# Two skewed streams of 512-token tiles, with weights cast once to bf16 in DRAM, in a two-layer hybrid encoder

## The chip, the cores and the metric

The kernel runs on the 8 cores of one Trainium2 chip. Each core takes two of the sixteen sequences, 4096 tokens in all, and runs the same program; no core waits for another. The metric is the device time of the slowest core, in microseconds.

## What is computed

x is (16, 2048, 1024) float32. Layer 0 mixes tokens by windowed attention, layer 1 by a gated short convolution; each is followed by a gated MLP whose gate goes through a width-3 convolution over positions.

```
def _conv_glu_ffn(h, w_gate_up, conv_w, w_down):
    gu = h @ w_gate_up                                   # (B, S, 2*D_FF), D_FF = 2816
    g, u = jnp.split(gu, 2, axis=-1)
    return (jax.nn.silu(_dwconv3(g, conv_w)) * u) @ w_down

def _short_conv_mixer(h, w_in, conv_w, w_out):
    b_gate, c_gate, xv = jnp.split(h @ w_in, 3, axis=-1)
    return (b_gate * _dwconv3(c_gate * xv, conv_w)) @ w_out

for i in range(2):
    hn = _rmsnorm(h, g_pre_mix)
    mix = _windowed_gqa(hn, ...) if i == 0 else _short_conv_mixer(hn, ...)
    h = h + _rmsnorm(mix, g_post_mix)
    f = _conv_glu_ffn(_rmsnorm(h, g_pre_ffn), ...)
    h = h + _rmsnorm(f, g_post_ffn)
```

Attention has 16 query and 4 key heads of width 64, rotary positions, a band of 128 tokens to each side and a learned sink.

## The kernel before

Activations lie channels by tokens, 128 channels a chunk, 8 chunks. The tokens of a core are cut in four stages of 1024 tokens; a stage is two tiles of 512 tokens (the last stage: three of 342). Both tiles of a stage go through the same steps one behind the other and share every weight that is loaded:

1. `wo_stage`: the attention's output projection (8 matmuls per chunk and tile), norm, residual from `xT`, result to the DRAM tensor `hd`.
2. `ffn` of layer 0: `pre_norm`, then 22 times a gate unit and an up unit of 8 matmuls each (`proj`), `conv3`, silu and product into `act`; then `down`, 22 matmuls per output chunk.
3. `conv_layer`: `pre_norm`, 8 times three units of 8 matmuls, then `down` with 8 matmuls per chunk.
4. `ffn` of layer 1, whose `down` writes the output `yT`.

Each of the four ends in `down` (L736 to L776) with the same tail, called a stage boundary here: the norm's factor `rs` on ScalarE, then for each of 8 chunks of each tile a residual load `hl` (256 KB, from `xT` or `hd`), a multiply and an add on VectorE, and a store of the chunk (256 KB); the next `pre_norm` squares the chunks, sums them on TensorE (`ones`), and scales them on VectorE, and only then can the next projections run. All of the tile's stages use one `x` and one `act` buffer.

Weights are float32 in DRAM. `load_w` (L463) loads a unit through GpSimd's DMA queue, which casts it to bf16 on the way, into a ring `w` of six. Residual loads, stores and attention's inputs `xs` are issued by SyncE (SP).

QKV projections and attention of the next stage's tiles are side work: `spread` (L883) gives them due times between those of the main line, on two PSUM banks of their own. The order on every engine is made by `Graph.schedule` (L182): a list scheduler with modelled durations that takes, on each engine, the ready operation with the earliest due time `vt`. ScalarE has a penalty of 15 for an operation that needs another function table. The program keeps that order: an engine runs its instructions strictly one after the other and waits for semaphores in place, and so does a queue's issuer.

The convolution needs tokens of the neighbour tile: `conv3` copies two columns in (`gs<-hs`) and two out (`hs<-gs`) for each tile and unit, on VectorE (L706, L708).

Attention for tiles 0 and 1 is all done before the first stage starts.

## Time and profile before

| | |
|---|---|
| three runs | 3545.93, 3550.9, 3839.99 us; median 3550.9 |
| the profiled execution | 3548.72 us; the span of its slowest core (core 3) 3547.2 us |
| spans of the eight cores | 3509.2 to 3547.2 us |
| busy, of the span | TensorE 89%, VectorE 55%, ScalarE 50%, GpSimd 12% |
| mean granted clock of TensorE | 0.929 of full speed on core 3 |

TensorE (PE) is the busiest engine. A busy share is a mean over stages of very different kinds, so the rows further down are cut by stage. The granted clock has two levels in the records, 1.0 (2.4 GHz) and 0.5 (1.2 GHz); a fraction between them is a window that holds both. "Share" of DMA is the mean busy share of the core's 16 DMA engines. GB/s counts bytes written: a load that casts float32 to bf16 reads twice of what it is counted for.

### The profile page before, as it was taken

To read this page: it belongs to the slowest core of one execution; us is meant where nothing else is said; L and a number is where in the kernel's file an instruction comes from. 1 tells how busy PE (TensorE), PEld (TensorE's weight loads), DVE (VectorE), ACT (ScalarE), POOL (GpSimd) and SP (SyncE) were. 2 spreads that over 40 slices of the span, in tenths; PEclk is the share of its full clock that TensorE was granted. 3 is DMA by queue.
4 is the path that set the end of the run, shared out by engine and by line. 5 is a ranking of instruction groups with operands and counts; after the bars stand their busy time and mean duration, and the time that the engine had idled before them with its cause. 6 is when DMAs were issued, how large, how long until landed. Compare 5 with 4: busy or idle time off the path is not lost.

```text
span 3547.2 us, 49902 instructions; the slowest of 8 cores (3509.2 to 3547.2 us)
## 1 busy us (share of the span) xinstructions
PE 3145.1 (89%) x14720; PEld 1406.1 (40%) x14720; DVE 1947.3 (55%) x4030; ACT 1774.4 (50%) x3095; POOL 425.1 (12%) x807
## 2 busy tenths in 40 slices
PE   3598999888998799897999799988999699888995
PEld 1212444333433344342443234433343256554663
DVE  3443771747724674465752577174872477175742
ACT  1276554455555455445556354445555565335641
POOL 1100111111110111010111011111111011110110
PEclk8757999999999899898999899989999899998997
DMA  6803574656547756646654965465543855555544
GB/s 146 164 6 85 111 130 68 144 87 126 79 62 172 164 95 110 137 75 140 117 95 57 201 127 76 65 146 94 120 74 55 177 106 76 90 127 138 82 73 113
DMA packets 219624, 382.13 MB, mean 108 GB/s; under 512 B 26210, under 2 KB 60002, under 8 KB 219362
## 3 DMA queue, kind: packets, MB, share of 16 engines
q0 software_dynamic: 115200, 205.57, 39.1%
q1 hardware_dynamic: 104162, 173.37, 17.8%
q8 instruction: 126, 2.06, 0.2%
q14 instruction: 136, 1.11, 0.1%
HBM read 516.47 MB, written 67.90 MB: 165 GB/s over the span
## 4 chain that ended last, share of the span: by engine, by line
PE 75%; DMA 11%; DVE 5%; ACT 4%; issue 3%; SPq 1%; DVEq 0%; ACTq 0%; POOLq 0%
PE ps L294 75%; DMA hl<-hd 5%; DVE x L307 3%; DMA xs<-xT 2%; DVE x L317 1%; DMA yT<-x 1%; DMA hl<-xT 1%; DMA tabd<-t 1%; ACT rs L303 1%; ACT pt L303 1%; DMA cosT<-tabd 1%; ACT rec L303 1%; SPq L329 1%; ACT sq L303 1%; DVE gc L317 0%
## 5 line engine op out<-in xcount | busy, mean ns | idle before, releaser
L294 PE MATMUL ps<-x,w 128*128 128x512 bf16 (+3 forms) x8064 | 1648.4, 359 | 30.0 <-DVE x L317 19.2
L294 PEld LDWEIGHTS ps<-x,w 128*128 128x128 bf16 x8064 | 783.7, 98 | 834.2 <-issue 116.5
L294 PE MATMUL ps<-act,w 128*128 128x512 bf16 (+6 forms) x3744 | 800.2, 356 | 0.1
L317 DVE SCALAR_TENSOR_TENSOR gc<-gs,cst_sb,gc 128x512 f32<-128x512 f32 (+9 forms) x1018 | 659.6, 653 | 136.4 <-ACT gc L303 91.6
L294 PEld LDWEIGHTS ps<-act,w 128*128 128x128 bf16 x3744 | 354.2, 98 | 329.9 <-issue 33.7
L303 ACT ACTIVATE gc<-gs,cst_sb 128x512 f32<-128x512 f32 (+6 forms) x468 | 312.0, 670 | 180.9 <-DVE gs L321 161.9
L303 ACT ACTIVATE gs<-ps 128x512 f32<-128x512 f32 (+3 forms) x396 | 215.0, 545 | 282.7 <-PE ps L294 273.1
L303 ACT ACTIVATE sq<-ps 128x512 bf16<-128x512 f32 (+6 forms) x280 | 157.1, 562 | 389.2 <-PE ps L294 388.8
L303 ACT ACTIVATE act<-gc 128x512 bf16<-128x512 f32 (+5 forms) x396 | 229.8, 583 | 238.8 <-DVE gc L317 141.8
L294 PE MATMUL ps<-sq,ones 128*128 128x512 bf16 (+7 forms) x496 | 195.9, 397 | 149.0 <-ACT sq L303 145.7
L329 POOL DMA_DIRECT2D w<-wgu x352 | 185.8, 528 | 1164.0 <-PE ps L294 1163.9
L307 DVE TENSOR_TENSOR act<-act,ps 128x512 bf16<-128x512 bf16 (+5 forms) x396 | 248.1, 629 | 131.9 <-ACT act L303 88.3
L307 DVE TENSOR_TENSOR x<-x,rs 128x512 f32<-128x512 f32 (+6 forms) x280 | 166.4, 640 | 255.9 <-ACT rs L303 255.7
L303 ACT ACTIVATE pt<-ps 128x512 bf16<-128x512 f32 x368 | 214.8, 598 | 73.3 <-PE ps L294 69.5
L307 DVE TENSOR_TENSOR x<-x,hl 128x512 f32<-128x512 f32 (+6 forms) x280 | 177.7, 642 | 115.8 <-DMA hl<-hd 94.9
L294 PE MATMUL ps<-hns,wq 128*128 128x512 bf16 x640 | 185.9, 405 | 47.7 <-DVE hns L317 20.0
L307 DVE TENSOR_TENSOR q<-ps,rec 64x512 bf16<-64x512 f32 x128 | 87.4, 683 | 232.6 <-PE ps L294 122.8
L303 ACT ACTIVATE x<-ps,cst_sb 128x512 f32<-128x512 f32 (+6 forms) x280 | 181.8, 650 | 42.8 <-DMA yT<-x 40.8
L303 ACT ACTIVATE sq<-x 128x512 bf16<-128x512 f32 (+4 forms) x216 | 122.9, 581 | 159.7 <-DVE x L307 147.7
L294 PE MATMUL ps<-q,k 64*128 64x512 bf16 x368 | 160.6, 445 | 22.5 <-ACT pt L303 15.2
L329 POOL DMA_DIRECT2D w<-wd x192 | 101.3, 528 | 640.2 <-PE ps L294 640.2
L307 DVE TENSOR_TENSOR pt<-pt,mhi 128x512 bf16<-128x512 bf16 x120 | 50.9, 424 | 221.5 <-ACT pt L303 221.0
(69 smaller groups left out, 1967.9 us busy)
## 6 DMA issues: line engine op xcount, KB each, us to landing
w<-wgu POOLq DMA_DIRECT2D x352, 256.0 KB, 4.6
hd<-x SPq DMA_DIRECT2D x144, 256.0 KB, 5.5
xs<-xT SPq DMA_DIRECT2D x128, 256.0 KB, 6.2
w<-wd POOLq DMA_DIRECT2D x128, 256.0 KB, 4.1
hl<-hd SPq DMA_DIRECT2D x120, 256.0 KB, 6.9
w<-win POOLq DMA_DIRECT2D x96, 256.0 KB, 4.6
wq<-wqk POOLq DMA_DIRECT2D x80, 256.0 KB, 5.7
hl<-xT SPq DMA_DIRECT2D x64, 256.0 KB, 7.2
```

The lines of the kernel that those rows point to most:

```text
L294: return lambda e: e.matmul(out, lhsT=lhsT, rhs=rhs, start=start, stop=stop)
L303: return lambda e: e.activation(out=out, in_=in_, func=func, **kw)
L307: return lambda e: e.tensor_tensor(out=out, in0=in0, in1=in1, op=o)
L317: return lambda e: e.scalar_tensor_tensor(out=out, in0=in0, scalar=scalar, in1=in1, op0=o0, op1=o1)
L329: return lambda e: e.dma_start(out=out, in_=in_)
```

## The change

- The 4096 tokens are eight tiles of 512 tokens. Even tiles are stream 0, odd tiles stream 1. Each stream has its own `x`, `act`, conv buffers, three PSUM banks and a ring of five weight buffers, and loads every weight for each tile. The due times set stream 1 behind stream 0 by 28 us of its own matmul time (56 us where both run). The last tile is cut into two parts of 258 and 254 tokens.
- 188 DMAs on GpSimd's queue cast all weights once, from DRAM to bf16 tensors in DRAM, eight in flight: the ninth waits for the first. Weights are then loaded as bf16 by SP (`load_w`), except those of attention for the first tiles, which are not cast yet and still come through `load_f32`.
- The copies of edge columns go from VectorE to GpSimd.
- Attention of tile 1 and the QKV of tile 2 get due times beside the start of stream 0. The residual buffers `hl` are now the conv buffers of the stream; `xs` has two buffers in place of four.
- The penalty for a new function table is 3 in place of 15 except for attention's exponentials. In the scheduler's model each DMA queue has a rate of its own, 230 GB/s, where one of 260 was shared.
- `down` starts its matmuls on each third of a chunk's weights as it comes.

```
+XW = 516
+SKEW = 28.0
...
-                key = hp[0][0] + (15.0 if tab is not None and tab != table else 0.0)
+                key = hp[0][0] + (hp[0][2].pen if tab is not None and tab != table else 0.0)
...
-                dma_free = max(dma_free, e.free) + o.nbytes / 260e3
-                fin = dma_free + 2.0
+                fin = max(dma_free.get(e, 0.0), e.free) + o.nbytes / 230e3
+                dma_free[e] = fin
+                fin += 2.0
...
-        x = sb("x", [128, NCH, XW], F32)
-        xbf = x[:, :, :].bitcast(BF16)
-        act = sb("act", [128, NFF, XW], BF16)
-        hl_r = ring("hl", 4, [128, 512], F32, True)
-        gs_r = ring("gs", 3, [128, GSW], F32)
-        gc_r = ring("gc", 2, [128, 512], F32)
...
+        class Stream:
+            def __init__(self, i):
+                self.i = i
+                self.x = sb(f"x{i}_", [128, NCH, XW], F32)
+                self.xbf = self.x[:, :, :].bitcast(BF16)
+                self.act = sb(f"act{i}_", [128, NFF, XW], BF16)
+                self.gs = ring(f"gs{i}_", 2, [128, XW], F32, True)
+                self.yc = ring(f"gc{i}_", 2, [128, 512], F32, True)
+                self.hl = Ring([self.gs.items[0], self.yc.items[0], self.gs.items[1], self.yc.items[1]])
+                self.w = ring(f"w{i}_", 5, [128, 1024], BF16, True)
+                self.sq = ring(f"sq{i}_", 2, [128, 512], BF16)
+                self.rs = ring(f"rs{i}_", 1, [128, 512], F32)
+                self.xB = [[Buf() for _ in range(2)] for _ in range(NCH)]
+                self.actB = [[Buf() for _ in range(2)] for _ in range(NFF)]
+                self.frontB = [Buf() for _ in range(2)]
+                self.st = [[dsem(f"d_st{i}_{c}_{p}") for p in range(2)] for c in range(NCH)]
...
-        xs_r = ring("xs", 4, [128, 512], F32, True)
+        xs_r = ring("xs", 2, [128, 512], F32, True)
...
+        castB = {}
+
+        def cast_w(key, i, dst, src, n):
+            castB[key] = Buf()
+            op(POOL, f_dma(dst, src), 0.55, [], [castB[key]], dsem=cast_sems[i % 8], nbytes=512 * n)
+
+        def load_w(rg, key, src, n):
             it = rg.next()
-            op(POOL, f_dma(it.ap[:, 0:n], src), 0.55, [], [it.buf], dsem=it.dsem, nbytes=512 * n)
+            op(SP, f_dma(it.ap[:, 0:n], src), 0.06, [castB[key]], [it.buf], dsem=it.dsem, nbytes=256 * n)
+            return it
+
+        def load_f32(rg, src, n):
+            it = rg.next()
+            op(POOL, f_dma(it.ap[:, 0:n], src), 0.55, [], [it.buf], dsem=it.sw, nbytes=512 * n)
             return it
 
         def mm(out, lhsT, rhs, first, last, reads, wbuf, n):
...
+                        rb = [b for c in range(NCH) for b in st.xcells(c, pv.col, pv.col + pn)]
+                    op(POOL, f_copy(st.xbf[:, :, 2 * c0:2 * c0 + 1], src), 0.3, rb + cur, [st.frontB[si]])
...
+        def edge_in(ge, src, hrow):
+            op(POOL, f_copy(src.ap[:, 0:2], hs[:, hrow, :]), 0.3, [hsB[hrow]], [src.edge])
+
         def conv3(ge, src, hrow, wcol):
 
             s, n, na = src.ap, ge.n, ge.na
-            op(DVE, f_copy(s[:, 0:2], hs[:, hrow, :]), 0.12, [hsB[hrow]], [src.buf])
             if ge.w1 < NTOK:
-                op(DVE, f_copy(hs[:, hrow, :], s[:, n:n + 2]), 0.12, [src.buf], [hsB[hrow]])
+                op(POOL, f_copy(hs[:, hrow, :], s[:, n:n + 2]), 0.3, [src.buf], [hsB[hrow]])
             else:
-                op(DVE, f_memset(s[:, n + 2:n + 3], 0.0), 0.1, [], [src.buf])
+                op(POOL, f_memset(s[:, n + 2:n + 3], 0.0), 0.3, [src.buf], [src.edge])
             b0 = ge.sh + 1
-            y = gc_r.next()
+            y = ge.st.yc.next()
             d = y.ap
-            op(ACT, f_act(d[:, 0:na], s[:, b0 + 1:b0 + 1 + na], AF.Copy, scale=wcol(1)), t_act(na, True),
-               [src.buf, cstB], [y.buf])
+            rd = [src.buf, src.edge, cstB]
...
+        def down(st, subs, ph_lag, l, gj, nk, wsrc, movs, res, dst):
 
             info = []
-            for si, sub in enumerate(subs):
+            for sub in subs:
                 a0, a1 = sub.win(ph_lag)
-                info.append((sub, a0, a1 - a0, sub.pool.get()))
+                info.append((sub, a0, a1 - a0, st.pool.get()))
             for m in range(NCH):
-                slots = []
+                bks = [st.pool.get() for _ in subs]
                 for k0 in range(0, nk, 8):
                     kn = min(8, nk - k0)
-                    slots.append(load_w(w_r, wsrc(m, k0, kn), kn * 128))
-                for si, (sub, a0, n, ss) in enumerate(info):
+                    sl = load_w(st.w, *wsrc(m, k0, kn), kn * 128)
+                    for bk, (sub, a0, n, ss) in zip(bks, info):
+                        for k in range(k0, k0 + kn):
+                            for (lo, hi, mv, mb) in movs(sub, k, a0, n):
+                                mm(bk.ap[:, lo:hi], sl.ap[:, (k - k0) * 128:(k - k0) * 128 + 128], mv, k == 0,
+                                   k == nk - 1, [sl.buf] + mb, bk.buf, hi - lo)
+                    yield kn * t_mm(512)
+                for bk, (sub, a0, n, ss) in zip(bks, info):
...
+                    hl = st.hl.next()
+                    for (dst_ap, src_ap, nb, rb) in res(c, a0, n, hl.ap):
+                        op(SP, f_dma(dst_ap, src_ap), 0.06, rb, [hl.buf, hl.edge], dsem=hl.dsem, nbytes=nb)
...
+        def stream(st):
+            for t in range(st.i, 8, 2):
+                if t < 7:
+                    subs = [Sub(t, 512 * t, 512 * t + 512, 0, st.pool)]
+                else:
+                    st.pool.idle.extend(side_pool.idle)
+                    subs = [Sub(t, 3584, CUT7, 0, st.pool), Sub(t, CUT7, NTOK, 258, st.pool)]
+                yield from down(st, subs, 0, 0, 1, 8, lambda m, k0, kn: (("o", m), bo[m]), wo_movs, res_x, dst_h)
+                hook(t, "wo", 0)
+                yield from ffn(st, t, subs, 0)
+                yield from conv_layer(st, t, subs)
+                hook(t, "conv", 0)
+                yield from ffn(st, t, subs, 1)
...
+        first = Banks(bank)
+        spread(lambda: (a_norm(0, first), a_kv(0, first), a_q(0, first), a_norm(1, first), a_kv(1, first)), 0.0, 100.0)
+        spread(lambda: a_att(0, Banks(bank[0:3]), Banks(bank[3:5]), ()), 70.0, 60.0)
+        rest = Banks(bank[3:8])
+        spread(lambda: a_q(1, rest), 100.0, 30.0)
+        spread(lambda: (a_norm(2, rest), a_kv(2, rest)), 130.0, 30.0)
+        spread(lambda: a_att(1, Banks(bank[5:7]), Banks(bank[7:8]), ()), 130.0, 60.0)
+
+        g.vt = 0.0
+        i = 0
+        for (nm, dst, src, n_) in (
+                [(("o", m), bo[m], wo[m], 1024) for m in range(8)] +
...
+            g.vt = 40.0 + 2.0 * i
+            cast_w(nm, i, dst, src, n_)
+            i += 1
...
+        streams[0].pool, streams[1].pool = Banks(bank[0:3]), Banks(bank[3:6])
+        gens = [stream(streams[0]), stream(streams[1])]
+        at = [0.0, SKEW]
+        alive = [True, True]
+        end0 = 0.0
+        while alive[0] or alive[1]:
+            i = 1 if not alive[0] or (alive[1] and at[1] < at[0]) else 0
+            w = at[i]
+            if alive[0]:
+                g.vt = base + (w if w < SKEW else 2 * w - SKEW)
             else:
```

How the order moves. GpSimd's queue, in the middle of the first `down` of layer 0; before it holds nothing but weight loads (`w` numbers are ring slots, `wd` the down weights):

```order
L329 DMA w4<-wd 128x1024
L329 DMA w5<-wd 128x1024
L329 DMA w0<-wd 128x768
L329 DMA w1<-wd 128x1024
L329 DMA w2<-wd 128x1024
L329 DMA w3<-wd 128x768
```

And in the change, the end of the casts (`bd<-wd` casts down weights of layer 1; `gs0`, `gs1` are conv buffers of stream 0 and 1, `hs` the saved edges). The last cast stands behind the edge copies into `gs0` of all 22 units of the first tile's first FFN and of 7 units of the second tile:

```order
L336 DMA bd<-wd 128x1024
L328 COPY gs1_1<-hs 128x2
L336 DMA bd<-wd 128x1024
L328 COPY hs<-gs1_0 128x2
L336 DMA bd<-wd 128x768
L336 DMA bd<-wd 128x1024
L328 COPY hs<-gs1_1 128x2
L328 COPY hs<-gs0_0 128x2
L336 DMA bd<-wd 128x1024
L328 COPY gs1_0<-hs 128x2
L336 DMA bd<-wd 128x768
L328 COPY gs1_1<-hs 128x2
```

The edge copies of both streams stand in one queue behind the casts; each cast waits for the cast eight before it.

SP, at a stage boundary before (`x` to `hd` is the store of a chunk, `hl` the next residual load):

```order
L329 DMA hd<-x 128x511
L329 DMA hl2<-hd 128x511
L329 DMA hd<-x 128x511
L329 DMA hl3<-hd 128x511
L329 DMA hd<-x 128x511
L329 DMA hl0<-hd 128x512
```

And in the change, at the end of stream 0's conv layer (`x0` is its buffer, `w1` the weight ring of stream 1, `gs0` and `gc0` its residual buffers):

```order
L336 DMA w1_3<-bin 128x1024
L336 DMA w1_4<-bin 128x1024
L336 DMA hd<-x0_ 128x510
L336 DMA gs0_0<-hd 128x510
L336 DMA w1_0<-bout 128x1024
L336 DMA hd<-x0_ 128x510
L336 DMA gc0_0<-hd 128x510
L336 DMA w1_1<-bout 128x1024
L336 DMA hd<-x0_ 128x510
L336 DMA gs0_1<-hd 128x510
L336 DMA wq1<-bqk 128x1024
L336 DMA hd<-x0_ 128x510
```

The stores of stream 0, which wait for VectorE, now stand between the weight loads of stream 1, and there are 2234 rows on SP where there were 768. Instructions by engine, before and after: VectorE 4030 and 3077, SP 775 and 2267, GpSimd 803 and 1200, ScalarE's table loads 43 and 103, TensorE 14720 and 14792 matmuls. Up to the last cast TensorE has 1224 matmuls in the order, 448 of them of the FFN projections, and SP 231 transfers with 51.6 MB.

## Rows read from the trace of the kernel before

**Rows 1.** The profile's page: busy tenths and clock over 40 slices of the span.

```profile
span 3547.2 us, 49902 instructions; the slowest of 8 cores (3509.2 to 3547.2 us)
...
PEclk8757999999999899898999899989999899998997
DMA  6803574656547756646654965465543855555544
```

**Rows 2.** Windows: time, each engine's busy time (instructions), granted clock, DMA share, GB/s.

```profile
core 3: us, PE busy (x) PEld busy (x) DVE busy (x) ACT busy (x) POOL busy (x), PEclk, DMA share, GB/s
...
0.00:180.00 180.00, 83.31 (x313) 33.10 (x314) 76.51 (x143) 41.88 (x71) 22.01 (x43) 0.80 0.74 154
180.00:375.00 195.00, 167.55 (x465) 41.59 (x463) 84.33 (x154) 129.80 (x223) 5.80 (x11) 0.67 0.25 58
375.00:628.00 253.00, 252.84 (x1163) 111.41 (x1162) 133.75 (x270) 131.75 (x217) 40.13 (x77) 1.00 0.58 95
```

**Rows 3.** Windows: the eleven stage boundaries and the end, by time.

```profile
628.00:672.00 44.00, 34.72 (x123) 10.97 (x122) 39.43 (x72) 28.07 (x49) 2.07 (x4) 0.84 0.82 210
782.00:834.00 52.00, 31.62 (x111) 11.10 (x109) 38.83 (x69) 27.02 (x42) 2.64 (x5) 0.77 0.73 178
1086.00:1218.00 132.00, 93.04 (x358) 35.52 (x358) 75.02 (x121) 61.89 (x102) 10.54 (x20) 0.86 0.83 197
1460.00:1500.00 40.00, 27.44 (x88) 8.34 (x87) 29.19 (x52) 23.39 (x40) 1.58 (x3) 0.74 0.84 201
1622.00:1672.00 50.00, 31.06 (x112) 10.01 (x111) 37.41 (x67) 24.50 (x40) 2.47 (x5) 0.80 0.80 190
1942.00:2075.00 133.00, 99.97 (x359) 36.04 (x358) 81.97 (x141) 62.51 (x101) 12.15 (x23) 0.85 0.90 195
2302.00:2349.00 47.00, 36.16 (x120) 10.78 (x119) 38.47 (x71) 29.27 (x51) 1.58 (x3) 0.78 0.72 196
2460.00:2510.00 50.00, 31.43 (x117) 10.39 (x116) 36.26 (x67) 24.53 (x39) 2.11 (x4) 0.83 0.72 189
2766.00:2870.00 104.00, 69.20 (x297) 29.15 (x297) 60.06 (x113) 51.04 (x92) 6.86 (x13) 0.85 0.83 189
3086.00:3140.00 54.00, 35.58 (x195) 17.99 (x193) 42.12 (x102) 24.71 (x52) 3.17 (x6) 0.84 0.69 183
3238.00:3282.00 44.00, 27.05 (x130) 12.22 (x129) 36.52 (x88) 22.55 (x49) 1.58 (x3) 0.73 0.72 207
3500.00:3548.00 48.00, 6.89 (x46) 4.08 (x43) 21.57 (x48) 6.94 (x13) 0.00 (x0) 0.60 0.54 161
```

**Rows 4.** DMA view of 630 to 661 us, inside the first of these boundaries.

```profile
DMA  9996999999999998899999999999999999999999
DMA packets 4649, 8.47 MB, mean 273 GB/s; under 512 B 519, under 2 KB 2418, under 8 KB 4647
q1 hardware_dynamic: 4306, 7.85, 91.2%
q0 software_dynamic: 341, 0.60, 13.1%
```

**Rows 5.** The page's DMA queues: packets, MB, share of 16 engines' span.

```profile
q0 software_dynamic: 115200, 205.57, 39.1%
q1 hardware_dynamic: 104162, 173.37, 17.8%
```

**Rows 6.** The page's DMA issues: count, KB each, us to landing.

```profile
w<-wgu POOLq DMA_DIRECT2D x352, 256.0 KB, 4.6
hl<-hd SPq DMA_DIRECT2D x120, 256.0 KB, 6.9
```

**Rows 7.** Groups of instructions: count, busy us, mean ns, idle before.

```profile
L321 DVE COPY gs<-hs 128x2 f32<-128x2 f32 x468 | 83.1, 178 | 68.5 <-ACT gs L303 60.1 <-ACT gc L303 0.7 <-DVE gs L307 0.5
L321 DVE COPY hs<-gs 128x2 f32<-128x2 f32 x416 | 70.1, 169 | 35.0 <-DVE gs L321 1.2
L303 ACT ACT_TABLE_LOAD x43 | 55.2, 1283 | 17.6 <-DVE gc L313 4.9 <-PE ps L294 4.2 <-DMA sinks<-sink 4.1
```

368 lines of the change are left out of this document (181 added, 187 removed).

## The prediction

> **What bounds the kernel now.** I read the 40 slices first, then cut the span into stages, then looked at what DMA does where TensorE is short of work. The slices [rows 1] show a clock that drops at intervals and DMA that is full at the same places. The windows [rows 2] say why. From 375 to 628 us, one whole FFN for two tiles, TensorE is busy for 252.8 of 253 us at full clock: 1163 matmuls, 217.5 ns each. No other engine matters there. VectorE has 134 us of work, ScalarE 132, DMA is at 0.58. So a dense stage is TensorE's own, and nothing this change does makes it shorter.
>
> The time that can be won lies elsewhere. In the eleven stage boundaries and at the end [rows 3] the lengths add up to 798 us. The eight short ones, 40 to 54 us each, and the end (429 us in all) hold 671 matmuls of 512 columns and, in the last stage, 371 of 342 columns; at 217.5 ns and 145 ns (342/512 of it) that is 200 us of work, so 229 us are lost. The three long ones, where the next stage's output projection and the side work of attention also sit (132, 133 and 104 us), hold 1014 matmuls, 221 us, and lose 148. Together 377 us are lost. What ends last in a boundary is DMA: from 630 to 661 us the queues are never idle and move 8.47 MB [rows 4]. Nearly all of it belongs to the 16 residual loads and 16 stores of two tiles (256 KB each, 8.4 MB), and nothing can overlap them, since both tiles are at the same point.
>
> The start is the third part. By 375 us only 313 + 465 matmuls have run [rows 2], some 169 us of work, and 180 to 375 us has a clock of 0.67 and DMA at 0.25: attention on ScalarE.
>
> **The sum.** I cut the new span where the casts end.
>
> *Up to the last cast.* The order gives the cut: 1224 matmuls, 448 of them FFN. Before, this much work is done at 375 us (778 matmuls) plus 446 x 0.2175 = 97, so 472 us. Now DMA sets this time. Each cast waits for the one eight before it, and the edge copies stand in the same queue, so a stream that needs its copy waits for the casts ahead of it. What DMA must do by then, priced by the queue rows [rows 5]: q0 takes 39.1% of 3547 us for 205.57 MB, 6.75 us per MB written; q1 17.8% for 173.37 MB, 3.64 us per MB. The 188 casts write 48.2 MB: 325 us. The 28 attention units still loaded through GpSimd, 7.3 MB: 50 us. SP's 51.6 MB: 188 us. Sum 563 us with all 16 engines busy, and 7 us until the first cast: **570 us**. By bytes read instead, 96.4 + 14.7 + 51.6 = 163 MB at the 292 GB/s of the full boundary (7.85 MB of plain and twice 0.60 MB of casting traffic in 31 us) [rows 4] it would be 557. The earlier start of stream 0 beside attention of tile 1, which would save up to 100 us of the start, is used up by this: the start gets 98 us longer. No row shows a cast from DRAM to DRAM. The low bound is that it costs what its written bytes cost on q1, 175 us, so 420 in all. The high bound is one cast at a time at the 4.6 us that a casting load takes to land [rows 6], 865 us. I take the middle value because it is the price of the nearest row, the same cast with another target.
>
> Here I weigh a rule. Row first: while full, a core's DMA moved 292 GB/s of reads [rows 4]. The Trainium skill (HBM Reference, Specifications) gives each core of a pair about 358 GB/s when both stream. A DRAM-to-DRAM cast uses that share twice, 0.52 MB read and 0.26 written, so by the page the first part moves 211 MB and takes an estimated 590 us, and the sum would be 20 us higher.
>
> *The dense rest.* 3547 - 472 = 3075 us before, less the 377 lost: **2698 us**, unchanged. Loading bf16 for each tile costs DMA what casting for two tiles did: 2 x 3.64 against 6.75 us per MB, so dense stages keep their 0.58.
>
> *Boundaries.* One stream's boundary is 4.2 MB while the other stream computes. At full TensorE rate the other needs 0.262 MB per 8 matmuls, 1.74 us, or 151 GB/s. Of 292 that leaves 141, so the 4.2 MB take 30 us, and the other stream's next boundary is 56 us away. That hides the short ones except for moments in which a store waits for VectorE on SP and the other stream's weight loads wait behind it; five buffers are 8.7 us of work and a residual load takes 6.9 to land [rows 6], so the margin is thin. Of 188 us (229 less the 41 of the end) I keep a fifth: **37**. At the end of a tile three lots of 4.2 MB meet (residual of the output, of the projection, and `xs`), 89 us at 141 GB/s, more than the 56 between the streams; of 148 I keep half: **74**. Bounds: nothing, and all 336.
>
> *End.* Before 48 us with 46 matmuls. Now one stream is alone at the end and closes two parts of a tile: half of the tail's transfers, so **35** with what the lone stream idles.
>
> *Costed at nothing:* the edge copies that leave VectorE, 83 + 70 = 153 us of its time [rows 7], as VectorE is covered in dense stages. They come back on GpSimd, where only the casts ahead of them matter. 60 more table loads at 1283 ns [rows 7] are 77 us on ScalarE, which is free half of a dense stage; without that cover they would cost up to 77. SP issues 1492 more DMAs; nothing there is computed, but see the second rival.
>
> Sum 570 + 2698 + 37 + 74 + 35 = 3414 us, against the span of 3547. The profiled execution took 1.5 us beyond its span and the median is 2 us above it, so **3417 us**: 3.8% faster.
>
> **The rivals.** *Casts are cheap.* Only 16 long pieces each, and the late ones run beside dense work where DMA has 0.42 free. Then the first part ends near 440 and boundaries leave 75: 440 + 2698 + 75 + 35 + 3 = 3251. Against it: bytes, not pieces, set the price [rows 4, 5]. Chance 0.18.
>
> *The boundaries stay.* The order of each engine is fixed. If a boundary takes longer than was planned, TensorE stands at stream 0's first projection although stream 1 has work, and stream 1's weights stand behind stream 0's stores on SP. Then three quarters of 336, 252 us, are still lost: 570 + 2698 + 252 + 35 + 3 = 3558, no change. For it: full queues [rows 4] and a landing time of 6.9 us against 8.7 us of weights. Against it: the plan reckons with 230 GB/s where 292 were moved. Chance 0.25.
>
> *The casts hold the edge copies up*, the case on the other side. If casts go at 4.6 us each, the first part ends at 871 us and the sum is 871 + 2698 + 37 + 74 + 35 + 3 = 3718, 5% slower. It decides from where the median passes 3622 (2% above): the first part at 775, so casts at (775 - 245)/188 = 2.8 us each against 1.73. Chance 0.15.
>
> **Numbers.** Forecast 0.42, with a range of its own from 3330 to 3500; most of its spread is the first part. A measurement of this kernel tells from no change only what lies over 2%, below 3480 or above 3622. Faster: four fifths of the forecast, the cheap casts, and a tenth of the staying boundaries, 0.34 + 0.18 + 0.03 = 0.55. Slower: 0.13 + 0.03 = 0.16. The rest, 0.29, is the same. The range 3250 to 3620 holds the forecast, half of the cheap case, most of the staying boundaries and little of the slow one, about 0.78.
>
> **What would show it.** The time at which the last cast is issued, read on the DMA queues: 570 right, 440 or over 770 wrong. DMA share near 1.0 until then, and TensorE with holes that end with a GpSimd copy or a weight load. After it, clock at 1.0 throughout and windows of 100 us with over 95 us busy, with one shallow dip per 85 us at most. If dips of 20 us stay, the second rival holds. Table loads should count 103 and show in no wait of TensorE. The forecast is wrong if the casts cost other than 1.2 to 2.3 us each, or if a lone stream cannot feed TensorE at full rate from five buffers.

## The result, and the profile after

The changed kernel is slower: a median of 3646.4 us against 3548.4 us for the kernel before on the same chip, a ratio of 1.028 (95% interval 1.026 to 1.030). The forecast was 3417 us in a range of 3250 to 3620, and the chance given to slower was 0.16. The profiled execution took 3645.8 us with a span of 3644.3. Some executions were disturbed and are left out of every ratio here, so a ratio can differ from that of two medians. Every ratio is to the kernel before on the same chip; the experiments ran on five chips, on which the kernel before takes 3549 to 3563 us, so the difference of two profiled spans can be off by some 15 us.

The page of the changed kernel, the same rows as [rows 1]:

```profile
span 3644.3 us, 54175 instructions; the slowest of 8 cores (3610.7 to 3644.3 us)
...
PE 3113.9 (85%) x14792; PEld 1419.0 (39%) x14792; DVE 1811.9 (50%) x3077; ACT 1854.1 (51%) x3173; POOL 351.0 (10%) x1204
...
PEclk9657688799999999999999999999999999999998
DMA  9688889975555557665566567655555564565555
...
q1 hardware_dynamic: 319010, 552.01, 52.4%
q0 software_dynamic: 15424, 55.59, 12.0%
```

Read the two lines of digits together. The intervals at which the clock dropped in [rows 1] are gone, and DMA is even at 0.5 to 0.7, except in the first eight slices: there DMA is mostly at 0.8 to 0.9 and the granted clock at 0.5 to 0.9. The queue rows, beside [rows 5], give q0 12.0% of 3644 us for 55.59 MB, 7.87 us per MB; it was 6.75 for loads that cast on the way to the chip's own memory.

The last cast is issued at 726.6 us. So I cut there. The windows of the changed kernel (columns as in [rows 2]):

```profile
0.00:375.00 375.00, 139.15 (x420) 42.65 (x420) 88.16 (x172) 88.31 (x150) 63.59 (x127) 0.74 0.83 131
375.00:726.00 351.00, 218.40 (x788) 78.55 (x788) 135.35 (x215) 163.63 (x253) 62.31 (x154) 0.78 0.92 158
726.00:3000.00 2274.00, 2177.86 (x9684) 919.23 (x9684) 1245.37 (x1997) 1284.41 (x2100) 165.64 (x622) 0.98 0.60 175
3000.00:3645.00 645.00, 578.45 (x3900) 378.61 (x3900) 343.06 (x695) 317.71 (x672) 59.45 (x302) 0.95 0.56 167
...
0.00:800.00 800.00, 419.75 (x1496) 149.80 (x1497) 259.91 (x439) 280.91 (x451) 131.77 (x306) 0.77 0.86 148
1400.00:2600.00 1200.00, 1158.68 (x5160) 488.08 (x5158) 671.28 (x1067) 680.56 (x1108) 91.32 (x334) 0.99 0.61 180
```

And the same stretches of the kernel before:

```profile
0.00:472.00 472.00, 347.70 (x1221) 118.05 (x1222) 235.19 (x447) 226.47 (x384) 45.21 (x87) 0.79 0.51 104
0.00:800.00 800.00, 655.28 (x2568) 245.03 (x2568) 400.41 (x761) 392.42 (x659) 86.37 (x165) 0.86 0.54 105
1400.00:2600.00 1200.00, 1104.54 (x4764) 452.43 (x4763) 687.84 (x1350) 614.21 (x1013) 149.02 (x283) 0.95 0.59 110
```

420 + 788 = 1208 matmuls are done at 726 us. Before, 1221 were done at 472. The first part costs 254 us more. The rest takes 3644 - 726 = 2918 us where it took 3547 - 472 = 3075, 157 less. 254 - 157 = 97 us, the whole difference of the spans. In 1400 to 2600 us the change runs 5160 matmuls in place of 4764: what it was made for works there. Everything hangs on the first 726 us.

What TensorE waits for there (us in total, times, longest), in 0 to 726 us of the changed kernel:

```profile
PE ps L301 <- ACT sqs L310: 120.7, 13, 37.4
PE ps L301 <- DVE hns L324: 60.1, 17, 10.9
PE ps L301 <- DMA w<-bgu: 56.7, 6, 18.4
```

`sqs` and `hns` are the norm of attention's input, worked out from the loads `xs`; so the inputs of attention cost more than the weights. How long the loads take is seen in the DMA view of 0 to 726 us (issues: count, KB each, us to landing):

```profile
DMA  8999848918997959986979987966999999999999
...
q0 software_dynamic: 14740, 54.49, 58.7%
q1 hardware_dynamic: 27736, 49.58, 28.0%
...
bgu<-wgu POOLq DMA_DIRECT2D x88, 256.0 KB, 11.9
w<-bgu SPq DMA_DIRECT2D x61, 256.0 KB, 12.5
xs<-xT SPq DMA_DIRECT2D x60, 256.0 KB, 8.2
```

The same plain load over the whole run (the page's DMA issues):

```profile
w<-bgu SPq DMA_DIRECT2D x704, 256.0 KB, 3.0
```

A plain weight load lands 12.5 us (median) after its issue beside the casts and in 3.0 us over the run. A ring of five is used up in 8.7 us of work. The timeline at 613 us (start, length, instruction, in brackets the idle time before it and what ended it) shows the end of one such load. Its issue is at 583.00, so it took 30 us:

```profile
583.00 0.32 SPq L336 DMA_DIRECT2D w<-bgu  x1
```

```profile
613.04 0.58 PE L301 MATMUL ps<-x_,w 128*128 128x511 bf16 x1 [18.39 <-DMA w<-bgu]
```

TensorE stood still for 18.39 us, and a load of 256 KB ended it. The chain of waits up to 760 us says the same of the inputs of attention, which come through a ring of two (start, length, what):

```profile
by line: PE ps L301 28.7%; DMA xs<-xT 20.8%; DMA w<-bgu 8.5%; DMA tabd<-t 7.6%; DMA cosT<-tabd 7.3%; issue 3.6%; ACT pt L310 2.8%; DMA gc<-xT 2.5%; ACT rec L310 2.3%; DMA w<-bo 2.1%; DMA gs<-xT 2.0%; SPq L336 1.9%; ACT L310 1.2%; DVE hns L3
...
50.72 31.17 DMA xs<-xT
...
179.23 17.73 DMA xs<-xT
197.81 18.38 DMA xs<-xT
...
583.00 29.91 DMA w<-bgu
```

TensorE is 29% of this chain. DMAs of 256 KB and less, one after the other, make up half of it (51%).

### The profile page after: what moved, and what is told of

Its sections match the earlier page's. It is cut to its first block, busy times and chain, and to the rows that moved or that the text cites. A ratio compares the mean times of both kernels' runs of the same rounds, so it can differ in the third digit from the quotient of the medians.

```text
span 3644.3 us, 54175 instructions; the slowest of 8 cores (3610.7 to 3644.3 us)
## 1 busy us (share of the span) xinstructions
PE 3113.9 (85%) x14792; PEld 1419.0 (39%) x14792; DVE 1811.9 (50%) x3077; ACT 1854.1 (51%) x3173; POOL 351.0 (10%) x1204
## 3 DMA queue, kind: packets, MB, share of 16 engines
q0 software_dynamic: 15424, 55.59, 12.0%
## 4 chain that ended last, share of the span: by engine, by line
PE 73%; DMA 15%; ACT 4%; DVE 4%; issue 3%; SPq 1%; POOL 0%; DVEq 0%; ACTq 0%; POOLq 0%
PE ps L301 73%; DMA xs<-xT 4%; DMA w<-bgu 3%; DMA tabd<-t 2%; DMA cosT<-tabd 2%; DMA gs<-hd 1%; DVE x_ L314 1%; SPq L336 1%; DMA gc<-hd 1%; DVE gc L324 1%; ACT pt L310 1%; DMA gs<-xT 1%; ACT L310 1%; DVE x_ L324 1%; ACT rec L310 1%
## 5 line engine op out<-in xcount | busy, mean ns | idle before, releaser
L301 PE MATMUL ps<-x_,w 128*128 128x512 bf16 (+6 forms) x8064 | 1704.9, 363 | 118.8 <-DMA w<-bgu 71.6
L301 PEld LDWEIGHTS ps<-x_,w 128*128 128x128 bf16 x8064 | 787.1, 99 | 925.5 <-issue 238.1
L324 DVE SCALAR_TENSOR_TENSOR gc<-gs,cst_sb,gc 128x512 f32<-128x512 f32 (+10 forms) x1018 | 655.5, 652 | 523.1 <-ACT gc L310 484.8
L301 PE MATMUL ps<-act_,w 128*128 128x512 bf16 (+6 forms) x3744 | 816.6, 356 | 2.1 <-DMA w<-bd 1.1
L301 PEld LDWEIGHTS ps<-act_,w 128*128 128x128 bf16 x3744 | 354.4, 97 | 341.4 <-issue 34.4
L310 ACT ACTIVATE gs<-ps 128x512 f32<-128x512 f32 (+4 forms) x396 | 215.4, 548 | 445.5 <-PE ps L301 437.2
L314 DVE TENSOR_TENSOR act_<-act_,ps 128x512 bf16<-128x512 bf16 (+5 forms) x396 | 246.0, 627 | 227.8 <-PE ps L301 119.8
L310 ACT ACTIVATE act_<-gc 128x512 bf16<-128x512 f32 (+5 forms) x396 | 226.6, 578 | 181.5 <-DVE gc L324 179.1
L314 DVE TENSOR_TENSOR x_<-x_,rs 128x512 f32<-128x512 f32 (+8 forms) x288 | 168.4, 627 | 93.2 <-ACT rs L310 92.7
L310 ACT ACTIVATE x_<-ps,cst_sb 128x512 f32<-128x512 f32 (+8 forms) x288 | 183.6, 637 | 12.2 <-DMA yT<-x_ 10.6
## 6 DMA issues: line engine op xcount, KB each, us to landing
bgu<-wgu POOLq DMA_DIRECT2D x88, 256.0 KB, 11.9
```

What stands on the lines that cost most here:

```text
L301: return lambda e: e.matmul(out, lhsT=lhsT, rhs=rhs, start=start, stop=stop)
L310: return lambda e: e.activation(out=out, in_=in_, func=func, **kw)
L314: return lambda e: e.tensor_tensor(out=out, in0=in0, in1=in1, op=o)
L324: return lambda e: e.scalar_tensor_tensor(out=out, in0=in0, scalar=scalar, in1=in1, op0=o0, op1=o1)
```

## The experiments

Theory A of the first runs: the 188 casts lengthen the start by the DMA time that they take, and the dense rest is as seen. Its rivals are named in the expectations. Three things had to be told apart: how much the casts cost, by what (bytes, pieces, waiting, the copies on GpSimd's queue), and what still costs TensorE time after them. All ratios are to the kernel before.

**One cast of each kind.** Eight casts are left of 188; the bf16 loads keep their number and bytes.

```
+            if unit(key) != key:
+                return
...
-            op(SP, f_dma(it.ap[:, 0:n], src), 0.06, [castB[key]], [it.buf], dsem=it.dsem, nbytes=256 * n)
+            op(SP, f_dma(it.ap[:, 0:n], one[unit(key)]), 0.06, [castB[unit(key)]], [it.buf], dsem=it.dsem, nbytes=256 * n)
```

> The changed kernel with 8 casts in place of 188: one unit of each weight tensor is cast (two sizes for the down weights), and every bf16 load of that tensor reads this one unit, so the output is not the reference's. All bf16 loads, rings and queues stay. Theory A (the first 725 us go to the casts: 437 us of 16 engines on their queue, and plain loads that land 12 to 30 us late beside them): 1224 matmuls are done near 450 us instead of 725, and the time is 3340 to 3420. Rival B (the start is lost by the new order of attention, two xs buffers in place of four and table loads): at most 60 us better, 3580 to 3640. Rival C (two streams wait for each other later on): the part after 725 us stays at 2919 us in either case; it can be read off the same run.

Measured: 0.955 (0.952 to 0.957). Windows of this kernel:

```profile
0.00:485.00 485.00, 331.09 (x1203) 116.00 (x1204) 222.71 (x386) 252.71 (x402) 40.72 (x100) 0.84 0.55 124
0.00:800.00 800.00, 634.74 (x2546) 243.19 (x2547) 388.27 (x646) 414.61 (x668) 57.69 (x171) 0.90 0.58 143
```

2546 matmuls by 800 us where the change had 1496 and the kernel before 2568. The work of the first part is done at 485 us, and the rest takes 3408 - 485 = 2923, as in the change (2918). So the 180 casts cost (1.028 - 0.955) x 3548 = 259 us by the ratios and 236 by the two profiled spans, and of the spans' difference all is in the first part (726 - 485 = 241). Theory A and Rival C hold, Rival B does not. TensorE's waits up to 485 us in this run:

```profile
PE ps L301 <- ACT sqs L310: 48.7, 12, 24.2
PE ps L301 <- DVE hns L324: 24.6, 13, 4.9
PE ps L301 <- DMA w<-bgu: 5.2, 3, 2.7
```

With the casts these three are 159 us longer. The second thing in these rows: without casts the start is no shorter than before, 485 against 472. Attention of tile 1 beside stream 0's start gains nothing on balance; whether the ring `xs` of two in place of four takes the gain away was not tried.

**Pieces of 2 KB.** The DRAM tensors of the casts get a pitch of 1280 in place of 1024 elements, so that a cast is 128 pieces of 2 KB in place of 16 of 16 KB. This holds for 140 of the 188; the 48 casts of down weights wrote rows of their own before too.

```
-    bgu = nc.dram_tensor("bgu", [2, 44, 128, 1024], BF16).ap()
+    bgu = nc.dram_tensor("bgu", [2, 44, 128, 1280], BF16).ap()[:, :, :, 0:1024]
```

> The changed kernel with the bf16 copies in DRAM at a row pitch of 1280 in place of 1024, so that a cast goes as 128 pieces of 2 KB and not as 16 of 16 KB. Same bytes, same count, same order rule. Theory A1 (a 16 KB piece holds a DMA engine for 2.0 us and every plain 2 KB piece behind it waits): plain loads land in 5 to 8 us during the casts, the holes of the first 700 us shrink, and the time is 3520 to 3590. Rival A2 (only bytes matter): 3630 to 3660.

Measured: 1.028 (1.025 to 1.030), as Rival A2 has it. Twice the packets on the queue, 15680 more (140 x 112), at nearly the same share of DMA time (the page's DMA queues; 12.0% before this edit):

```profile
q0 software_dynamic: 31104, 55.59, 12.6%
```

The plain load `w<-bgu` lands in 14.0 us in the first part against 12.5. It does not wait because the pieces ahead of it are long. The Trainium skill (DMA: Bandwidth & Descriptors, Queues, rings and completion order) says that a DMA engine takes turns between its queues a packet at a time, and that a packet typically holds some 9 to 17 descriptors. If a piece is one descriptor, a cast leaves each of the 16 engines 16 KB to do in one turn, as one piece or as eight; by that the size of a piece would not matter, and the run agrees. What an engine takes in one turn no run here shows.

**Loads that read one unit, all 188 casts made.** The run with one cast of each kind, with the casts put back: no plain load waits for any but the first casts, and DMA has as much to do as in the change. Against that run:

```
-            if unit(key) != key:
-                return
```

> The changed kernel with all 188 casts, at the same places in GpSimd's queue, but every bf16 load reads the first unit of its tensor, so that no load waits for any but the first casts; the output is not the reference's. With eight casts alone the time was 3407 us. Theory A3 (the casts cost DMA time that the streams need, whoever reads them): 3600 to 3650, as if they were read. Rival A4 (the streams wait for the casts that they read, and would run ahead if they had not to): 3400 to 3480.

Measured: 1.028 (1.022 to 1.033), as Theory A3 has it, and 1507 matmuls by 800 us, as in the change. The casts cost by being there, not by being waited for.

**Half of the casts, unread.** The edit of the run before, and every second cast left out (94 remain):

```
+            if unit(key) != key and i % 2:
+                return
```

> As the run in which all 188 casts go out and nothing but the first unit of each tensor is read, but with every second cast left out: 94 in all; the output is not the reference's. With 8 casts the time is 0.9547 of the kernel before, with 188 it is 1.0276. Theory A5 (the start is bound by DMA's work, so each cast costs its share): 0.985 to 0.997. Rival A6 (there is room for half of them in DMA's idle time): under 0.975.

Measured: 0.997 (0.995 to 0.999), at the upper end of Theory A5; Rival A6 is out. With 8, 94 and 188 casts the ratio is 0.955, 0.997 and 1.028. The first 86 cost 150 us, the next 94 cost 108. The windows, two of this run and one of the changed kernel:

```profile
0.00:400.00 400.00, 147.45 (x438) 44.94 (x438) 96.37 (x185) 93.98 (x160) 64.03 (x128) 0.74 0.84 132
400.00:622.00 222.00, 191.48 (x771) 72.38 (x772) 128.78 (x207) 160.24 (x245) 19.09 (x60) 0.92 0.50 138
...
0.00:400.00 400.00, 146.87 (x439) 44.82 (x439) 96.37 (x185) 94.20 (x160) 66.07 (x132) 0.73 0.83 134
```

Half of the casts are not half as dense. GpSimd's order puts them as close together as before, the last one goes out at 381 us, and up to 400 us the two kernels are alike: 438 and 439 matmuls, DMA at 0.84 and 0.83. The run with one cast of each kind has 861 by then. Once the casts are over, the other 771 matmuls of the first part take 222 us. So the streams go at half to two thirds of their pace for as long as casts go out.

How they go out shows on GpSimd's queue in the changed kernel (one of its waits in 0 to 726 us, and two rows of the timeline):

```profile
POOL wq L336 <- PE ps L301: 252.1, 23, 43.8
...
169.34 3.86 POOL L336 DMA_DIRECT2D bgu<-wgu  x8
...
221.65 0.54 POOL L336 DMA_DIRECT2D wq<-wv  x1 [29.25 <-PE ps L301]
```

The casts leave in bursts, in the fixed order between the float32 loads `wq` of attention and the edge copies, and these wait for the streams. GpSimd waits 252 us for TensorE to free a buffer of `wq`, and 68 us for casts ahead of a cast. When a burst makes the inputs of attention late, TensorE is late, then GpSimd stands too, and DMA runs dry. So the time of the last cast follows the streams, and not the DMA time of the casts.

Is it the capacity of DMA or the longer landing of each load? DMA's busy time in the first part is 0.55 x 485 = 267, 0.72 x 622 = 448 and 0.87 x 726 = 632 us for 8, 94 and 188 casts. With 94 it is less than the 485 us that the first part takes without casts, and yet 622 us go by; so the sum of DMA's work does not give the time. What the loads meet inside a burst has to count as well. Whether they land late there because the engines are full, or whether it hurts only because they follow one another through short rings, the runs do not tell apart: one with two casts in flight in place of eight was not made, and neither was one with longer rings. From 500 to 726 us of the changed kernel DMA is at 0.97, and there its capacity is a limit in any case.

**Edge copies back on VectorE.**

```
-            op(POOL, f_copy(src.ap[:, 0:2], hs[:, hrow, :]), 0.3, [hsB[hrow]], [src.edge])
+            op(DVE, f_copy(src.ap[:, 0:2], hs[:, hrow, :]), 0.17, [hsB[hrow]], [src.edge])
```

> The changed kernel with the edge copies back on VectorE; GpSimd's queue holds DMAs alone. Theory F (the edge copies stand behind the casts in one queue and hold the streams): 3560 to 3600. Rival G (the streams are short of DMA, and GpSimd's copies mostly wait for the streams): 3630 to 3670, a little worse for 150 us more on VectorE.

The edit takes the copies out (`hs<-gs`) and those at the front of `pre_norm` back as well. Measured: 1.039 (1.035 to 1.043), worse than the change by 1.1% and than both theories said. 1210 matmuls are done at 775 us, where the change has 1208 at 726, so most of the loss is in the first part. There the last cast goes out earlier, at 667 us. The copies on GpSimd are a gain, though a copy takes longer there than the 169 and 178 ns of [rows 7]. The page's groups of the changed kernel:

```profile
L328 POOL COPY gs<-hs 128x2 f32<-128x2 f32 x468 | 119.4, 257 | 1286.3 <-DVE gc L324 629.7
L328 POOL COPY hs<-gs 128x2 f32<-128x2 f32 x416 | 103.5, 249 | 1319.5 <-ACT gs L310 1041.7
```

GpSimd is idle before them, 1286 and 1319 us in all, and waits for the streams. With no copy behind a cast the kernel is slower, not faster: the rival "the casts hold the edge copies up" is wrong in its mechanism. It is rather the copies that hold the casts back. That this is why they are better on GpSimd, and not VectorE's relief, is possible and was not tested.

**No casts from DRAM to DRAM.** Stream 0's first use of a unit loads it in float32 through GpSimd, cast on the way into its ring, and SP stores the ring's bf16 to DRAM for all later uses. Attention of tile 0 loads float32. The bytes read fall; the writes to DRAM stay.

```
+            if key not in castB:
+                op(POOL, f_dma(it.ap[:, 0:n], f32src[key]), 0.55, [], [it.buf], dsem=it.sw, nbytes=512 * n)
+                i = len(castB)
+                castB[key] = Buf()
+                op(SP, f_dma(src, it.ap[:, 0:n]), 0.06, [it.buf], [castB[key]], dsem=cast_sems[i % 8], nbytes=256 * n)
+                return it
```

> No casts from DRAM to DRAM. Stream 0 loads each weight of its first tile as float32 through GpSimd's casting queue into its ring, and SP stores the bf16 copy from there to DRAM; all later uses load that copy. A weight costs 6.75 us per MB for the load and 3.64 for the store in place of 7.9 for the cast and 3.64 for a load. Theory A: about 70 us of DMA work less and, more important, nothing runs ahead of the streams, so the start is like that of the kernel before: 3400 to 3480. Rival D (the store on SP waits for the load to land, and what stands behind it on SP waits too): 3550 or more.

Measured: 0.969 (0.966 to 0.972), 3448 us: faster than both kernels, as Theory A has it. The DMA queue of its casting loads, from its page:

```profile
q0 software_dynamic: 28800, 51.39, 10.2%
```

51.39 MB for 10.2% of 3459 us are 6.86 us per MB, near the 6.75 of [rows 5]; the same cast with DRAM as its target was 7.87. Of the 259 us that the casts cost, (1.028 - 0.969) x 3548 = 209 are back (185 by the profiled spans). The first part (1218 weight loads of TensorE) is done at 500 us, 226 earlier, and the rest takes 3459 - 500 = 2959 us, 41 more than in the change. The casting loads of layer 1 now lie there, beside its first tile: DMA is at 0.80 from 726 to 1400 us where the change has 0.59, and TensorE waits 11.6 us for `w<-wgu`. (This trace misses some 2% of the matmuls, so its weight loads, the PEld column, are counted.)

**What still costs time after the start.** The rest of 2918 us is 74 above the 2844 of the forecast. First the parts of the change that could be at fault, each put back alone. The skew of the streams (in the changed kernel 28 to 1.7; in the write-back kernel 28 to 42, and 28 to 22):

```
-SKEW = 28.0
+SKEW = 1.7
```

> The changed kernel with the second stream due 1.7 us behind the first in place of 28, so that both tiles reach a stage boundary together. Theory A (the skew hides the boundaries, about 150 us of what the kernel before lost): 3760 to 3840. Rival E (the streams wait for each other whatever the skew, and what was gained after 725 us comes from own buffers and from VectorE's relief): 3620 to 3680.

> The write-back version with the second stream due 42 us behind the first in place of 28. Its dips between stages are some 5 us each. Theory J (the dips come from the length of one boundary's own chain, not from two boundaries that meet): 3430 to 3470, no change. Rival K (the three lots of transfers at the end of a tile meet the other stream's next boundary): 3390 to 3420.

> The write-back version with 22 us of skew in place of 28. At 42 it lost 2.7%, at 1.7 the changed kernel lost 4.5%. Theory P (a broad best place between, where no two boundaries of the streams meet): 0.965 to 0.975. Rival Q (28 is a lucky place of the fixed order, every other one loses): 0.98 or more.

Measured: without skew 1.073 (1.071 to 1.076); 42 in the write-back kernel 0.995 (0.992 to 0.998); 22 there 0.974 (0.971 to 0.977), against 0.969 with 28. Theory A of the skew and Theory P hold. The skew is worth 0.045, some 160 us, and nearly all of it is after the start: without it 1173 matmuls are done at 726 us, only 35 fewer, but 1400 to 2600 us holds 4777 in place of 5160. Neither theory had foreseen the loss with 42. That kernel runs 4943 in place of 5087 weight loads of TensorE in 1400 to 2600 us, so it loses there too, and it loads 141 function tables in place of 103; whether the tables are the cause is open.

The penalty for a new table, back to 15 everywhere (in the changed and in the write-back kernel):

```
-    def op(self, eng, fn, dur, reads=(), writes=(), dsem=None, nbytes=0, tab=None, after=(), pen=3.0):
+    def op(self, eng, fn, dur, reads=(), writes=(), dsem=None, nbytes=0, tab=None, after=(), pen=15.0):
```

> The changed kernel with the old penalty of 15 for every change of ScalarE's function table, so fewer table loads than 103. Theory H (the 60 loads more lie beside other work): 3630 to 3680, unchanged or a little worse, since the norm's two exponentials come later. Rival I (a table load stands twice in each dip between stages and costs 1.3 us each time): 3580 to 3610.

> The write-back version with the penalty of 15 for every table change: 97 table loads in place of 103. Theory T (table loads lie beside other work): 0.965 to 0.975. Rival U (they lie in the dips): 0.955 to 0.963.

Measured: 1.031 (1.022 to 1.039) against 1.028, and 0.967 (0.961 to 0.972) against 0.969. No difference. The scheduler still makes 95 and 97 loads of a table in place of 103, so the edit took few of them away, and what all 60 added ones cost was not measured.

Then the traffic of a boundary, in the write-back kernel. Four of the eight residual loads of a tile are left out where the residual comes from `hd`; and, apart from that, all residual loads and stores are issued by GpSimd, off SP's queue of weight loads:

```
+                    if c >= 4 and res is res_h:
+                        hl = Item(hns0[:, 0:512])
```

```
-                        op(SP, f_dma(dst_ap, src_ap), 0.06, rb, [hl.buf, hl.edge], dsem=hl.dsem, nbytes=nb)
+                        op(POOL, f_dma(dst_ap, src_ap), 0.55, rb, [hl.buf, hl.edge], dsem=hl.dsem, nbytes=nb)
```

> The write-back version without the residual loads of chunks 4 to 7 from the DRAM state at 23 of the stage ends of the tiles (VectorE adds other data in their place, at the same length; the output is not the reference's). These are the loads that no free buffer can take before the boundary begins. The write-back version stands at 0.969 of the kernel before. Theory L (the dips that are left between stages end with these loads, 5 to 7 us each): 0.935 to 0.95. Rival M (the dips come from the chain on ScalarE and VectorE and from the fixed order): 0.96 to 0.97.

> The write-back version with residual loads and stores issued from GpSimd's queue in place of SP's, so that no weight load stands behind a store that waits for VectorE. Theory N (that coupling on SP is a part of what is left): 0.955 to 0.963 of the kernel before. Rival O (SP's order costs nothing, and GpSimd's issue of 0.5 us and its casting loads of the first pass are dearer): 0.97 to 0.985.

Measured: 0.960 (0.957 to 0.964) and 0.979 (0.977 to 0.981), against 0.969. Rivals M and O hold. Half of the loads is worth 0.9%, and GpSimd's queue makes it worse by 1%. Taking the stores out of the way of the weight loads gains nothing that outweighs the price of GpSimd's queue; the run does not part the two.

What was left to try is the order itself. It is computed ahead with a modelled delay of 2 us between the end of a transfer and its use. The timeline of the write-back kernel at a stage boundary shows what follows:

```profile
1707.24 0.69 DVE L314 TENSOR_TENSOR x_<-x_,gs 128x512 f32<-128x512 f32 x1 [0.80 <-DMA gs<-hd]
...
1708.03 0.63 ACT L310 ACTIVATE sq<-x_ 128x512 bf16<-128x512 f32 x1 [1.70 <-DVE x_ L314]
...
1708.80 0.38 PE L301 MATMUL ps<-sq,ones 128*128 128x512 bf16 x1 [1.01 <-ACT sq L310]
...
1710.66 1.23 PE L301 MATMUL ps<-hns,wq 128*128 128x512 bf16 x4 [1.48 <-DVE t L314]
```

VectorE waits 0.80 us at the add for a residual load, `sq` behind it waits, and TensorE, in its fixed order, stands at a matmul of `ones` for 1.01 us. Then it stands 1.48 us for `t`, the side work of attention, which VectorE does after that add. Residual loads land 5.0 us after their issue in this run (median; up to 16.3), so a plan with 2 us puts the add too early; that is my reading of the timeline. So the delay in the model was set to other values; the code on the chip differs only in its order.

```
                 dma_free[e] = fin
-                fin += 2.0
+                fin += 5.0
```

> The write-back version, its order made with a fixed DMA delay of 5.0 us in the scheduler's model in place of 2.0; nothing else. Theory R (TensorE stands in dips because the order puts one stream's boundary work before the transfers it needs have landed): 0.95 to 0.962 of the kernel before, where the write-back version has 0.969. Rival S (the dips are of other origin, and a plan with more delay keeps weights back for nothing): 0.966 to 0.985.

> The same with a modelled delay of 0.5 us. Theory R: worse than the write-back version, 0.975 to 0.99. Rival S: 0.963 to 0.973.

> The write-back version with a modelled DMA delay of 8 us. Theory V (landing times of 3 to 5.4 us are covered by 5, more brings nothing): 0.945 to 0.965 of the kernel before. Rival W (every us more gives slack): below 0.945.

Measured in the write-back kernel: 0.5 us 0.985 (0.979 to 0.991), 2 us 0.969, 5 us 0.951 (0.946 to 0.957), 8 us 0.972 (0.968 to 0.976). Theory R holds twice; 8 us lies outside both its theories. What TensorE waits for in 1400 to 2600 us (sum, times, longest), with 2 us:

```profile
PE ps L301 <- ACT sq L310: 21.9, 15, 3.8
PE ps L301 <- DMA w<-bgu: 5.5, 5, 3.6
```

and with 5 us:

```profile
PE ps L301 <- DVE act_ L314: 9.6, 6, 2.9
PE ps L301 <- ACT sq L310: 7.5, 9, 2.4
```

The wait for the norm's squares falls by 14.4 us and the one for weights is gone from the top, but VectorE's `act` comes up by 7.4, and the seven longest waits together fall only from 41.2 to 35.1 us. In these 1200 us TensorE does 5160 weight loads in place of 5087, which is 16 us of work. Most of the 74 us between the two spans is won earlier: at 1400 us the kernel with 5 us is 5052 weight loads far and the other 4822, 50 us of work. With 8 us the gain is lost again and the ratio cannot be told from that with 2; why is open. Four delays are also four different orders, and the skew of 42 shows that an order can lose 2.6% for a reason that was not found; that 5 us is right because it is the landing time is therefore argued.

The same in the changed kernel and in the kernel before (there the line is `fin = dma_free + 2.0`):

> The changed kernel, casts and all, with a modelled delay of 5 us. Theory X (the two causes add: the casts' 7 to 8% stay, 1.8% is won after them): 1.005 to 1.017 of the kernel before. Rival Y (while the casts run, the order matters more, since loads land after 12 us and more): below 1.0.

> The kernel before, with a modelled delay of 5 us in place of 2. Theory Z (its boundaries are full DMA queues with both tiles at the same point, so no order helps): 0.99 to 1.005. Rival AA (it gains as the streams do): 0.975 to 0.985.

Measured: the changed kernel 1.010 (1.005 to 1.015) in place of 1.028, as Theory X has it; the kernel before 1.007 (1.005 to 1.009) in place of 1, a little above Theory Z. So the gain is seen in both kernels with two streams and not in the one without. That one stream has no other work that a late transfer could hold up would explain it, and is not shown. Windows of the changed kernel with 5 us:

```profile
0.00:722.00 722.00, 355.14 (x1202) 120.73 (x1203) 221.27 (x383) 247.88 (x396) 124.87 (x277) 0.77 0.89 148
...
800.00:3590.00 2790.00, 2652.86 (x13219) 1258.53 (x13217) 1543.34 (x2631) 1562.58 (x2712) 232.14 (x894) 0.99 0.60 176
```

1202 matmuls by 722 us: the start is as it was. The rest is 3588 - 722 = 2866 us in place of 2918. Of these 52 us, 26 are less time in which TensorE is not busy (162 and 136 us), the others busy time: from 726 to 1400 us the granted clock is 1.00 in place of 0.97. The two effects add up: write-back takes 0.059 off the change, the delay 0.018, and both together 0.076. Write-back with 5 us, 0.951, is the best version found: its profiled span is 3385.5 us.

## Why the prediction was wrong, step by step

**The first part, where it failed.** The step is "Up to the last cast: 570 us". Measured: 726. Its sum was DMA's work at the prices of the kernel before, with all 16 engines busy until the last cast, and both the price and the full overlap were off. The busy time, by the queue rows of 0 to 726 us, is 0.587 x 726 = 426 us for q0 and 0.280 x 726 = 203 for q1, 629 in place of 563. Per MB that is 7.82 and 4.10 us where I took 6.75 and 3.64 from [rows 5]; for the 54.49 and 49.58 MB moved by then it makes 58 and 23 us, and 15 fewer because 3 MB less were moved. The other 97 us are time in which DMA was not busy, of which I had put in 7. 58 + 23 - 15 + 97 - 7 = 156, what was missing. What the runs show in place of the sum: for as long as casts go out the streams go at half to two thirds of their pace, whoever reads the casts. The order ties the last cast to the streams: GpSimd waits 252 us for TensorE at `wq` and 68 us for casts, where I had taken the wait for the cast eight before as what sets the time. Up to 500 us DMA is at 0.83, which makes 85 of the 97 us; only after that is it full (0.97). A plain weight load lands after 12.5 us and not 3.9 (the first part of the run with one cast of each kind). The likely reason is that loads follow one another through a ring of two (`xs`) or five (`w`), so that each late one stops the rest; the run with 94 casts fits it (448 us of DMA work, 622 us of time), and no run tests it alone. I had read in [rows 6] that a residual load takes 6.9 us, and had used it for the boundaries only.

The rule that I weighed beside this, 358 GB/s for each core of a pair (HBM Reference, Specifications, in the Trainium skill), made an estimated 590 us of the first part. It erred the same way, as it also divides bytes by a rate; nearer, but 136 us short.

The bound of 865 us was too high: a cast of `bgu` took 11.9 us to land, but up to eight were in flight. By the prediction's own formula the casts came to (726 - 245) / 188 = 2.56 us each, against its 1.73 and outside the 1.2 to 2.3 that it named. It is below the 2.8 at which the slow rival was to decide. The formula takes the casts for what their queue waits for, which they were not. With the rest as forecast, 726 + 2844 + 2 = 3572 us would have been 0.7% slower; that it became 2.8% is the doing of the rest, 74 us too long. The slow rival's mechanism, casts that hold the edge copies up, is refuted by the run with the copies on VectorE, so the 0.15 stood for a mechanism that did not act. A detail of the cheap rival is wrong too: only 140 of the 188 casts are 16 long pieces.

**"Used up by this".** The saving of up to 100 us from the earlier attention was never there: without casts the first part takes 485 us, against 472. What the casts add to a start without them is 726 - 485 = 241 us. The forecast added 98 (570 - 472), since it let DMA's whole work lie under TensorE's and ScalarE's time.

**Boundaries and end, mis-sized.** 37 + 74 + 35 = 146 us forecast. Measured 2918 - 2698 = 220, if the dense work is 2698; 162 of them are time in which TensorE is not busy. 52 of the 74 us too many go with the other plan (2866 with 5 us). My reasons for the 37 were stores on SP ahead of weight loads, for which the run on GpSimd's queue shows nothing, and late residual loads, half of which are worth 0.9%. The second rival said that 252 of the 336 us of the boundaries stay. Less the 32 of the end, 188 stay: about halfway between the 111 of the forecast and the rival. In kind the rival is right, as TensorE does stand although the other stream has work; where the timeline shows it, it goes by VectorE's and ScalarE's order.

**The end.** 35 forecast. TensorE has nothing at all in the last 25 us and 12.83 us of work in the 20 before (windows of the changed kernel):

```profile
3600.00:3620.00 20.00, 12.83 (x107) 9.85 (x105) 4.14 (x12) 5.20 (x15) 0.00 (x0) 0.95 0.46 112
3620.00:3645.00 25.00, 0.00 (x0) 0.00 (x0) 7.64 (x20) 0.70 (x2) 0.00 (x0) 0.50 0.41 129
```

45 - 12.8 = 32 us lost. This term was right.

**What was right.** Dense stages are TensorE's own, and bf16 loads for each tile do not disturb them: DMA stays at 0.60, and TensorE is busy for 96% of 726 to 3000 us. The two streams win 157 us of the 377 that were lost after the start, and without the skew (160 us) all of it would be gone. 103 table loads in place of 43 show in no wait of size. The copies on GpSimd cost nothing, and are even worth 1.1%, for whichever reason. The sign was wrong because of the start alone: with the first part at 570 the same kernel would have taken 156 us less, 0.984 of before; with the rest at 2844 too it would have been at the forecast.

**The chances.** I gave 0.15 to one slow mechanism, and no case of its own to a first part between some 650 us, where the forecast's own range up to 3500 ends, and 775. It came out there. The landing times of casts, inputs and weights grow together, and I let none of them grow.

## What to carry to other kernels

Price a bulk transfer in the background twice: by the DMA time that it takes, and by what it does to the landing of the small loads beside it times the number of them that follow one another. Look for the place in the kernel where loads are in series through short rings, mostly the start, and keep bulk work out of it; a use that loads the data anyway can cast it and write it back. And where an order is fixed ahead of time with two streams in it, try the delay that the planner gives a transfer: here 5 us, near the 3 to 6 us in which loads and stores land in the trace, was 1.8% better than 2 in two kernels, and 8 was no better than 2.

## What the runs showed of the hardware that was not expected

- The queue with the casts from DRAM to DRAM takes 7.87 us of 16 engines per MB written (28 loads to the chip's memory among them), the same queue with the chip's memory as the only target 6.86 (the write-back kernel). Part of the difference can be the load beside it: plain transfers take 4.10 us per MB in the first 726 us of the changed kernel and 3.46 over its run.
- Pieces of 16 KB or of 2 KB in 140 of the 188 casts make no difference to the kernel's time, and little to the casts (12.0 and 12.6% of DMA) and to the weight loads beside them (12.5 and 14.0 us to landing).
- Casts with up to eight in flight raise the landing of a plain 256 KB weight load about three times, from 3.9 to 12.5 us in the first part, and one of them took 30 us. The 16 engines are meanwhile busy for 0.83 of the first 500 us, and for 0.97 of the time from there to the last cast.
- Residual loads and stores on GpSimd's queue in place of SP's cost 1%, with no casts left beside them but those of first uses.
